# Weight chunks in pairs: 1 MB transfers with 8 KB lines in a hybrid decoder step

## What is computed

```
xn = rms_norm(x, norm_w)
aq, ak, av, az, mq, mk, mv, mo, mz, ga, gm, mi, mf = split(xn @ w_in)
attn = moba_prompt(aq, ak, av)       # samples: moba_sample over cache_k, cache_v by page_table
h, (c, n, m) = mlstm(mq, mk, mv, gates)
h = rms_norm(h * sigmoid(mo), mh_norm_w)
y_att = (attn * silu(az)) @ w_proj_attn
y_ml = (h * silu(mz)) @ w_proj_mlstm
y = x + (sigmoid(ga) * y_att + sigmoid(gm) * y_ml) @ w_out
```

## Time and profile before

| | us |
|---|---|
| median of 3 runs | 469.26 |
| lowest, highest | 468.48, 469.58 |
| span of the profiled execution | 467.2 |
| TensorE busy | 456.2 |
| VectorE busy | 394.1 |
| ScalarE busy | 294.4 |
| GpSimd busy | 100.9 |

### The profile page before, as it was taken

One profiled execution on the slowest core, in us unless ns is written; L12 is line 12 of the kernel. 1 busy time (PEld: TensorE's weight loads), 2 busy tenths in 40 slices (PEclk: granted clock), 3 DMA queues, 4 the chain that ended last, 5 costly groups with the idle time before them and its releaser, 6 DMA issues.

```text
span 467.2 us, 11345 instructions
## 1 busy us (share of the span) xinstructions
PE 456.2 (98%) x3855; PEld 413.8 (89%) x3855; DVE 394.1 (84%) x1610; ACT 294.4 (63%) x490; POOL 100.9 (22%) x181
## 2 busy tenths in 40 slices
PE   6999999999999999999999999999999999999997
PEld 4899899897879888888899889899898898899997
DVE  3898899699999799999899999799999774668861
ACT  4966545686984496995486695666948357324430
POOL 2040421013323213423321332321223110000000
PEclk9999999999999999999999999999999999999999
DMA  8899699749999999999999999998999985457511
GB/s 304 322 353 407 183 322 371 240 158 340 317 416 408 404 368 354 412 410 408 408 380 315 409 412 409 411 372 303 382 415 409 410 334 188 149 180 261 182 48 48
DMA packets 44858, 150.91 MB, mean 323 GB/s; under 512 B 6192, under 2 KB 7796, under 8 KB 44672
## 3 DMA queue, kind: packets, MB, share of 16 engines
q1 hardware_dynamic: 20368, 70.77, 40.8%
q0 software_dynamic: 19008, 67.20, 37.3%
q10 hardware_dynamic: 5424, 12.21, 6.8%
HBM read 137.37 MB, written 12.76 MB: 321 GB/s over the span
## 4 chain that ended last, share of the span: by engine, by line
PE 70%; ACT 10%; DVE 10%; DMA 4%; issue 4%; ACTq 1%; POOLq 0%; SPq 0%; POOL 0%; DVEq 0%
PE pj L534 28%; PE pj L537 13%; PE wk L534 6%; PE pa L717 4%; PE wk L537 3%; DMA kpages<-in_cache_k 3%; DVE kpages L1170 3%; DVE wlo L1071 2%; ACT L838 2%; ACT whi L818 2%; PE wk L487 2%; DVE cslot L1252 2%; PE wk L639 2%; PE wk L673 1%; DMA cst<-in_consts 1%
## 5 line engine op out<-in xcount | busy, mean ns | idle before, releaser
L534 PE MATMUL pj<-xn,whi 128*128 128x264 f32 x1328 | 180.8, 288 | 1.6 <-ACT mqT L976 1.3
L534 PEld LDWEIGHTS pj<-xn,whi 128*128 128x128 f32 x1328 | 168.4, 189 | 10.2 <-issue 6.2
L1071 DVE TENSOR_TENSOR wlo<-wraw,whi 128x1024 fp32r<-128x1024 f32 x112 | 136.1, 1220 | 8.8 <-ACT whi L818 8.3
L818 ACT ACTIVATE whi<-wraw 128x1024 fp32r<-128x1024 f32 x112 | 117.9, 1053 | 23.1 <-PE wk L537 12.9
L1170 DVE CUSTOM_DVE_ANT_0 kpages<-kpages,qbc 128x128 f32<-128x128 f32 x512 | 115.5, 292 | 5.3 <-DMA kpages<-in_cache_k 5.1
L537 PE MATMUL pj<-xn,wlo 128*128 128x264 f32 x664 | 93.8, 284 | 0.4 <-DVE wlo L1071 0.4
L537 PEld LDWEIGHTS pj<-xn,wlo 128*128 128x128 f32 x664 | 85.5, 188 | 0.6 <-DVE wlo L1071 0.6
L404 POOL DMA_DIRECT2D kpages<-in_cache_k x64 | 34.3, 536 | 165.9 <-DVE sco L1170 141.9
L404 POOL DMA_DIRECT2D vpages<-in_cache_v x64 | 33.9, 530 | 57.9 <-issue 38.9
L1170 DVE DVE_READ_ACCUMULATOR2_ANT sco<- 128x1 f32 x512 | 42.8, 84 | 0.0
L717 PE MATMUL pa<-vpages,prob 128*32 128x256 f32 x512 | 34.2, 385 | 1.7 <-ACT prob L876 1.7
(11 more groups left out here) (271 smaller groups left out, 615.0 us busy)
## 6 DMA issues: line engine op xcount, KB each, us to landing
wraw<-in_weights SPq DMA_DIRECT2D x112, 512.0 KB, 6.8
kpages<-in_cache_k POOLq DMA_DIRECT2D x64, 512.0 KB, 8.1
vpages<-in_cache_v POOLq DMA_DIRECT2D x64, 512.0 KB, 10.8
cslot<-in_states SPq DMA_DIRECT2D x16, 512.0 KB, 9.4
out_C_s<-cslot ACTq DMA_DIRECT2D x16, 512.0 KB, 8.1
xres<-in_tokens SPq DMA_DIRECT2D x1, 1056.0 KB, 5.5
out_k_p<-kT ACTq DMA_DIRECT2D x4, 256.0 KB, 10.2
out_v_p<-v_nat ACTq DMA_DIRECT2D x4, 256.0 KB, 4.7
```

What stands on the lines that cost most here:

```text
L534: mm(bank[:, 0:T], whi[:, q, k, :], src[:, g, k, :], start=(k == 0 and g == 0), stop=False)
L818: A(whi[:, n % WSPLIT], wraw[:, n % WRAW], ACT.Copy).then_inc(whi_ready, 1)
L1071: V.tensor_tensor(wlo[:, n % WRAW], wraw[:, n % WRAW], whi[:, n % WSPLIT], ALU.subtract).then_inc(wlo_ready, 1)
```

## The change

The host lays the weights out by pairs of chunks: one line holds the two chunks' 8 x 128 numbers one behind the other, 8 KB. Chunks 0 to 3 are still loaded one at a time (load_half), each from one half of the long lines, with a semaphore of its own. From chunk 4 on load_w takes an even n and loads chunks n and n+1 into two slots that lie side by side, in one transfer of 1 MB. It waits until projection n-7 is done, since the second slot comes free then. Both splits of a pair wait for the one semaphore. Everything else, the order on the other engines too, is as before.

```diff
 WRAW = 8
+FIRST = 4
 WSPLIT = 4
...
-        wload = [sem(f"wload{i}") for i in range(WRAW)]
+        wload = [sem(f"wload{i}") for i in range(WRAW // 2)]
+        wfirst = [sem(f"wfirst{i}") for i in range(FIRST)]
...
                 if n >= WRAW:
-                    sp.wait_ge(proj, n - WRAW + 1)
-                sp.dma_start(wraw[:, n % WRAW].rearrange("p k c -> p (k c)"), a["weights"][n]).then_inc(wload[n % WRAW], 16)
+                    sp.wait_ge(proj, n - WRAW + 2)
+                w = n % WRAW
+                sp.dma_start(wraw[:, w:w + 2].rearrange("p n k c -> p (n k c)"), a["weights"][n // 2]).then_inc(wload[w // 2], 16)
+
+            def load_half(n):
+
+                sp.dma_start(wraw[:, n].rearrange("p k c -> p (k c)"),
+                             a["weights"][n // 2][:, n % 2 * KC * P:(n % 2 + 1) * KC * P]).then_inc(wfirst[n], 16)
...
-            for n in range(4, HEADS):
+            for n in range(FIRST, HEADS, 2):
                 load_w(n)
             for j in range(JOBS):
                 for k in range(len(GROUPS)):
-                    for half in range(2):
-                        load_w(HEADS + CHUNKS * j + 2 * k + half)
+                    load_w(HEADS + CHUNKS * j + 2 * k)
...
-                for c in range(KC):
+                for c in range(0, KC, 2):
                     load_w(HEADS + BODY + KC * m + c)
...
-                act.wait_ge(wload[n % WRAW], 16 * (n // WRAW + 1))
+                if n < FIRST:
+                    act.wait_ge(wfirst[n], 16)
+                else:
+                    w = n % WRAW
+                    act.wait_ge(wload[w // 2], 16 * (n // WRAW + (w >= FIRST)))
...
-    return np.concatenate([c.reshape(KC, P, 2, P).transpose(2, 1, 0, 3).reshape(2, P, KC * P) for c in cuts])
+    return np.concatenate([c.reshape(KC, P, 2, P).transpose(1, 2, 0, 3).reshape(1, P, 2 * KC * P) for c in cuts])
```

More of the change, by code:

```diff
@@ L345, in _ @@
             sp.dma_start(wg[:, :, :].rearrange("p k g -> p (k g)"), a["gate_weights"]).then_inc(boot_g, 16)
-            load_w(0)
+            load_half(0)
             sp.dma_start(bg[:, :], a["gate_bias"]).then_inc(boot_g, 16)
-            load_w(1)
-            load_w(2)
-            load_w(3)
+            for n in range(1, FIRST):
+                load_half(n)
             sp.dma_start(cst[:, C_FIRST:C_END], a["consts"][:, C_FIRST:C_END]).then_inc(boot_r, 16)
```

## The result

The changed kernel takes 472.09 us (median of 10 runs, 470.37 to 475.1) and the kernel before, run beside it, 469.42 us (10 runs, 468.48 to 470.2). The ratio is 1.0064 with a 95% interval of 1.0045 to 1.0084: slower, by 3.0 us (the two medians lie 2.7 us apart). The forecast was 469.2 us and no change, and 472.09 lies above its range, 468.3 to 471.0. The profiled execution took 471.93 us with a span of 469.8 us, 2.6 us longer than before's 467.2; the granted clock is full in both. Lines from L331 on are shifted: L537, L717, L1071, L1170, L1262 of before are L543, L723, L1081, L1180, L1272 now.

What follows compares the result with a forecast made beforehand. TensorE's own work was taken as the bound. Span 467.2 + 0 (Part 1) - 0.1 + 0 (Part 2) + 0 (the rest) = 467.1 us; with 2.1 us from span to median, 469.2 us, no change, range 468.3 to 471.0.

Steps and rivals of the forecast that it cites:

- What bounds the kernel: Whole span: TensorE's own work, busy 456.2 of 467.2 us; a transfer matters only through an engine TensorE then waits for.
- Part 1: Weight loads: even chunks start one projection (2.9 us) later, within the splits' margins of 9.0 and 11.5 us; cost zero.
- Part 2: Shared DMA queues: 8 KB lines give weights two thirds of the bytes against pages; zero for pages, -0.1 us for stores.
- the pages have the engines alone: About 3 us before each pair: pages undisturbed where the even chunk took half, a gain of up to 1.5 us.
- only their order changes: Weights and pages over a pair's period: the bytes are the same, only reordered.
- The key page of 354.05: Page ending VectorE's wait at 367.92: expected within half a microsecond of its place; bounds 0.9 us lost, 0.20 us gained.
- What counts is what weights were moved by the time a critical page lands: Page wait ending at 367.92: either kernel has moved chunks 86 and 87 by 367.9, so zero cost.
- The stores' term: State stores ScalarE awaits until 350.18, before the exponential TensorE awaits: -0.2 to +1 us, taken as -0.1.
- long turns starve the pages: Slower rival: key pages land 1.3 us later near 157 and 367.92 us, together +1.8, 471.0 us; chance 0.17.
- Late splits: Slower rival: ScalarE's splits wait for pairs landing over 9 us (end) or 11.5 (middle); +2, 471.3 us; chance 0.03.
- relief: Faster rival: larger lines relieve the full DMA engines, shrinking TensorE's waits by 2.1 us, 467.1 us; chance 0.08.

Runs made afterwards that it cites:

- the two places are mended: Against the kernel before: pairs with 8 KB lines everywhere but in the pairs of chunks 60, 62, 78 and 80, which have 4 KB lines; 470.35 us, 1.0021.

## Why the prediction was wrong, step by step

**What bounds the kernel.** Right: TensorE's work is unchanged, the transfers matter only through ScalarE, VectorE and GpSimd, and the DMA engines are as full as in the earlier trace rows (1.02, 404 GB/s from 327 to 374 us in both). But I read from TensorE's list alone who is near the path. GpSimd's list of before had the entry that decided (in the changed kernel it is 18.2, 4, 7.2):

```profile
POOL decay L433 <- DMA floor<-rows_dram: 10.2, 4, 3.9
```

**Part 1, cost zero.** Right for the splits: 7.8 us to landing in the median, estimated at 4.3 to 9.5 with 10.3 as the far bound (11.7 came, over that bound), and no wait of ScalarE for weights. From 400 us on, where the pairs are nearly alone, they land in 4.8 us in the median, against 4.3 in the estimate. What it left out is what the later start does to others. It was counted in Part 2 as a gain, "the pages have the engines alone"; near the rows this gain did not come: from 249 to 258 us the pages' queue moved less than before (0.89 MB against 1.49), and 1.5 us of the engines' time passed unused. That bytes come out the same over a pair's period, "and only their order changes", holds only while something is queued. With 4 KB lines the later start costs the median nothing that the runs can tell (1.0005, 0.9996).

**Part 2, the turns.** The mechanism was right: nearly equal turns, 82, 81 and 73 packets, and 0.67 MB against 0.30, two bytes for one. The Trainium skill (DMA: Bandwidth & Descriptors, Queues, rings and completion order) says that an engine drains some 9 to 17 descriptors of one queue before it turns to the next; the rotation read above, one line each, does not agree with it. The key page of 354.05 did not become the trouble, but the step that kept it in place was not exact either. It is asked for at 355.98 now and used without a wait at 368.1, so it takes at most 12.1 us in place of 13.85, which is more than the half microsecond allowed. Others are waited for, 1.05 us at 155.78, 0.81 at 360.79 and 1.44 at 372.41. In total VectorE's waits for key pages, 5.1 us in the earlier trace rows, are now 3.3.

```profile
DVE kpages L1180 <- DMA kpages<-in_cache_k: 3.3, 3, 1.4
```

**The step that failed is the choice of who is served after the weights.** "What counts is what weights were moved by the time a critical page lands": I asked that of the two key pages with a wait, and of no other load. The rows' loads, two of 1 KB, stand on the same queue behind three pages; with VectorE waiting 0.20 us for them already, any delay goes through to VectorE. This term, absent from the sum, is the larger one: 2.1 us by the medians (472.09 against 470.01 with the rows earlier) and 1.6 by the ratios, 1.9 in the profile.

**The stores' term was mis-sized.** I gave it -0.2 to +1 us and took -0.1, on the ground that the pair starts later. It measured +1.13 us in the profile (1.1 to 1.5 in five executions with long lines, two of them of the kernel itself) and some 1.5 us by the times (470.75 and 471.03 with long lines there alone, 469.27 and 469.49 without). Three queues were backlogged: a store's line then waits 159 + 309 ns for each turn instead of 159 + 159 (packet times in the trace; the prediction's 161 and 318 were close). The last store took 10.4 us from issue to landing against 9.2:

```profile
out_C_s<-cslot ACTq DMA_DIRECT2D x1, 512.0 KB, 10.4
```

**The sum made again**: +1.9 (rows) + 1.1 (stores) - 0.5 (given back after projection 78) + 0.1 = 2.6 us of span. **The rivals:** the slower one, long turns starve the pages, had the right cause and came near the time (471.0), but at the wrong place: its key pages are waited for less than before, that its figure comes near is luck. Late splits and relief did not come; larger lines could relieve little, with 309 ns for 8 KB against twice 159 for 4 KB, 3%. Not settled: how much of the late rows comes from the pair (the idle stretch, the packets driven apart) and how much from the long turns, since single executions scatter from 5.3 to 8.2 us with 4 KB lines; and whether the key pages of 360 us take over for good when the two places are mended (1.0021, with an interval that reaches 0.9999). The initial 0.3 us of the profile was not followed up; it comes and goes between the executions (-0.2 to +0.5 us).

## What to carry to other kernels

Where queues rotate by lines, the line's length is the queue's weight: doubling it takes service from every queue that is backlogged beside it, and here it sped up only what was not waited for. Before costing such a change, list every load and store that shares the engines, the 1 KB ones too, with the slack of its reader, from each engine's own waits and not from the bottleneck's alone. A load that starts later is no gain for the others unless they have something to move in that time. Repeat a run before you read a wait of a few microseconds out of one profiled execution.

## What the runs showed of the hardware

A backlogged engine takes its queues in turn, one line each, whether 8 KB, 4 KB or less (82, 81 and 73 packets from 346 to 349 us, 206 of 219 steps in order; 144 and 142 packets in the earlier trace rows, where the second queue's have 1 KB); a packet of 8192 bytes takes 309 ns and one of 4096 takes 159. Four of 54 transfers, in the two right stretches, bring the whole 0.6% (1.0063). Moving one wait out of the way (the stores') went with another on the next engine, 7.0 us of waits for key pages in place of 3.3. A load of 1 KB that is spread over 16 packets lands only with the last of them: with 4 KB pairs half of the packets came 6.2 us after the request and the last 10.5, against 6.5 and 7.8 before.
